# Picking expert tokens as rows by 512-column products, and expert comparisons moved beside a norm

## The reference

```python
g_w, g_idx = lax.top_k(softmax(xt @ w_group + b_group), 1)      # one of 4 groups
e_w, e_idx = lax.top_k(softmax(e_sel), 2)                       # 2 of its 4 experts
h = silu(einsum('nd,edf->nef', xt, w_gate)) * einsum('nd,edf->nef', xt, w_up)
h = h * combine[:, :, None]
y = einsum('nef,efd->nd', h, w_down)                            # D = 1024, F = 512
```

## Time and profile before

| | us |
|---|---|
| median of 3 runs | 1168.8 (1168.37 to 1170.16) |
| profiled execution | 1168.16 |
| its span | 1166.3 |
| PE busy | 1105.4 (95%) |
| DVE busy | 414.0 (36%) |
| ACT busy | 229.2 (20%) |

### The profile page before, as it was taken

One profiled execution on the slowest core, in us unless ns is written; L12 is line 12 of the kernel. 1 busy time (PEld: TensorE's weight loads), 2 busy tenths in 40 slices (PEclk: granted clock), 3 DMA queues, 4 the chain that ended last, 5 costly groups with the idle time before them and its releaser, 6 DMA issues.

```text
span 1166.3 us, 19793 instructions
## 1 busy us (share of the span) xinstructions
PE 1105.4 (95%) x8488; PEld 654.0 (56%) x8488; DVE 414.0 (36%) x1059; ACT 229.2 (20%) x531; POOL 128.3 (11%) x226
## 2 busy tenths in 40 slices
PE   4999999999899999999998899998999899999996
PEld 1666666666444576666654444444555656666562
DVE  2155656556712341000112655306863320000114
ACT  3111011011211321111111411115642411111110
POOL 0344434334100000000002000000000000000003
PEclk9999999999999999999999899999999999999999
DMA  9985444446842579999999920079770789999996
GB/s 346 291 292 149 136 146 146 146 146 217 338 187 89 180 270 423 411 428 427 424 427 348 368 102 1 18 258 371 263 281 18 253 353 418 429 426 424 425 418 227
DMA packets 102464, 321.27 MB, mean 275 GB/s; under 512 B 4048, under 2 KB 39168, under 8 KB 87008
## 3 DMA queue, kind: packets, MB, share of 16 engines
q1 hardware_dynamic: 93872, 298.05, 66.9%
q0 software_dynamic: 3248, 10.87, 2.8%
q10 hardware_dynamic: 5248, 10.98, 2.4%
HBM read 305.73 MB, written 14.16 MB: 274 GB/s over the span
## 4 chain that ended last, share of the span: by engine, by line
PE 80%; DMA 11%; DVE 4%; SPq 2%; issue 2%; ACT 1%; POOL 1%; POOLq 0%; ACTq 0%; DVEq 0%
PE bank L788 17%; PE bank L941 11%; PE bank L1181 11%; PE bank L811 7%; PE bank L678 7%; PE bank L777 6%; DMA ring<-in_moe_w_down 5%; PE bank L950 4%; PE bank L1067 4%; DMA ring<-in_w_ada 4%; PE bank L573 3%; PE bank L966 2%; PE bank L657 1%; DMA ring<-expert_rows,moe_row 1%; PE bank L664 1%
## 5 line engine op out<-in xcount | busy, mean ns | idle before, releaser
L788 PE MATMUL bank<-ring,xn 128*64 128x256 f32 x1472 | 163.5, 380 | 0.9 <-DMA ring<-in_moe_w_up 0.9
L788 PEld LDWEIGHTS bank<-ring,xn 128*64 128x64 f32 x1472 | 105.0, 137 | 61.4 <-issue 9.5
L941 PE MATMUL bank<-uT,ring 128*128 128x384 f32 x384 | 135.0, 496 | 0.0
L1181 PE MATMUL bank<-ring,uT 128*128 128x512 f32 x288 | 129.5, 603 | 4.3 <-DMA ring<-in_attn_w_qkv 2.7
L1869 DVE TENSOR_TENSOR moe_hh<-xn,bank 128x256 f32<-128x256 f32 x32 | 13.5, 421 | 291.7 <-ACT xn L1336 291.6
L811 PE MATMUL bank<-ring,xn 128*64 128x512 f32 x384 | 106.7, 596 | 0.9 <-ACT xn L1342 0.9
L941 PEld LDWEIGHTS bank<-uT,ring 128*128 128x128 f32 x384 | 69.2, 190 | 41.4 <-issue 1.1
L1181 PEld LDWEIGHTS bank<-ring,uT 128*128 128x128 f32 x288 | 54.1, 193 | 68.2 <-issue 64.1
L678 PE MATMUL bank<-ring,uT 128*128 128x512 f32 x192 | 84.1, 592 | 0.0
L777 PE MATMUL bank<-moe_g,moe_h 128*128 128x128 f32 x672 | 83.7, 282 | 0.5 <-DVE moe_g L1759 0.5
L777 PEld LDWEIGHTS bank<-moe_g,moe_h 128*128 128x128 f32 x672 | 79.9, 197 | 5.6 <-issue 5.6
(11 more groups left out here) (293 smaller groups left out, 1328.2 us busy)
## 6 DMA issues: line engine op xcount, KB each, us to landing
ring<-in_w_ada SPq DMA_DIRECT2D x24, 2048.0 KB, 12.1
ring<-in_moe_w_up SPq DMA_DIRECT2D x24, 2048.0 KB, 18.7
ring<-in_moe_w_gate SPq DMA_DIRECT2D x22, 2048.0 KB, 19.5
ring<-in_moe_w_down SPq DMA_DIRECT2D x21, 2048.0 KB, 19.9
ring<-in_hgrn_w_in SPq DMA_DIRECT2D x32, 512.0 KB, 6.9
moe_ring<-in_moe_w_gate SPq DMA_DIRECT2D x8, 2048.0 KB, 19.5
moe_ring<-in_moe_w_up SPq DMA_DIRECT2D x8, 2048.0 KB, 23.3
moe_ring<-in_moe_w_down SPq DMA_DIRECT2D x7, 2048.0 KB, 21.0
```

Of the source, the lines that this page charges most:

```text
L788: last = mm(bank[2 + e][64 * g:64 * g + 64, 256 * part:256 * part + 256], m["xe"][:, k, 64 * e:64 * e + 64], w[k][:, 256 * g:256 * g + 256 ...
L941: last = mm(to[:, 0:TOK], w[:, k, f, :], uT[:, k, :], start=(k == 0), stop=(k == KC - 1))
L1181: last = mm(bank[b % 2][:, :], uT[:, k, t * P:(t + 1) * P], cols(slot)[:, k, :], start=(k == 0), stop=(k == KC - 1))
```

## The change

It has two parts.

1. **Gather.** For pairs other than pair 1, `pick_rows(half, i)` now makes `moe_g` the stationary operand and `moe_h` the moving one: three products of 512 columns for each half give the picked tokens as rows (128 slots x 512 features) in bank 0 or 1. ACT (half 0) and DVE (half 1) copy them to `own[:, 1, :]` in the new step `picked`, and `gather(half, i)` then turns eight blocks of 128, as it did for pair 1 alone. `pick_rows(0, i+1)` stands behind the second gate/up product of pair i, `pick_rows(1, i+1)` behind the third; the turns stand where the gather stood. Pair 0 is picked and turned before the first body. POOL's fetch of pair 1 goes to the same place and waits until pair 0 has been turned. The counts of `gathered`, `xe_act` and `xe_dve` follow. (Further passes over the experts, which only a fuller expert needs, wait in `collect` for the slot of the last down weights.)
2. **Comparisons.** DVE's bias and comparisons are split by tiles: those of tiles 0 and 1 stand before the modulation of tile 2, their sums behind it, and only tile 2 is left for `experts`.

```diff
-GATHERS = 2 * PAIRS + FETCHED
+GATHERS = 4 * PAIRS - FETCHED
@@ PE, experts
+                def pick_rows(half, i):
+                    if half == 0:
+                        pe.wait_ge(s["onehot"], onehots_made(at_pass[0], i))
+                    for t in range(T):
+                        last = mm(bank[half][:, :], m["g"][:, t, :, :], m["h"][:, t, 512 * half:512 * half + 512],
+                                  start=(t == 0), stop=(t == T - 1))
+                    last.then_inc(s["gathered"], 1)
+
-                def gather(half, i):
+                def gather(half, i, it):
+                    if not fetched(i):
+                        pe.wait_ge((s["xe_act"], s["xe_dve"])[half], it * 2 + 1)
+                    elif half == 0:
+                        pe.wait_ge(s[f"rows{i}"], at_pass[0] * ROWS_IN[i] + 16)
                     for k in range(4):
-                        if 1 <= i <= FETCHED:
-                            here = slice((4 * half + k) * P, (4 * half + k + 1) * P)
-                            last = nc.tensor.transpose(bank[half][:, k * P:(k + 1) * P], m["own"][:, i, here], ident)
-                            continue
-                        for t in range(T):
-                            last = mm(bank[half][:, k * P:(k + 1) * P],
-                                      m["h"][:, t, (4 * half + k) * P:(4 * half + k + 1) * P],
-                                      m["g"][:, t, :, :], start=(t == 0), stop=(t == T - 1))
+                        here = slice((4 * half + k) * P, (4 * half + k + 1) * P)
+                        last = nc.tensor.transpose(bank[half][:, k * P:(k + 1) * P], m["own"][:, 1, here], ident)
                     last.then_inc(s["gathered"], 1)
@@ PE, body
                     gate_up(i, 0, 1, it)
+                    if picking:
+                        pick_rows(0, i + 1)
...
                     gate_up(i, 1, 0, it)
+                    if picking:
+                        pick_rows(1, i + 1)
                     if gating:
                         gate(n, m["diag"], 1, 2, 6)
                     gate_up(i, 1, 1, it)
                     if not last:
-                        gather(0, i + 1)
+                        gather(0, i + 1, it + 1)
@@ ACT, body
                         A(m["sg"][:, e, :], bank[2 + e][:, 0:256], ACT.Silu).then_inc(s["silu"], 1)
+                        if e == 0 and not last and not fetched(i + 1):
+                            picked(i + 1)
@@ DVE, second_norm and experts
                 second_norm(n, 2)
+                biased_logits(n, 0, 2)
+                compared(0, 2)
                 modulate(n, "xT2_done", "uT2_dve", 2, 1)
+                counted(0, 2)
...
-                need(dve, n, "logit_mm", 3)
...
+                biased_logits(n, 2, 3)
...
+                compared(2, 3)
+                counted(2, 3)
@@ POOL, fetch
+                        pool.wait_ge(s["gathered"], pair_gathered(p, 0, 1))
```

More of the change, by code:

```diff
@@ L843, in body @@
                 def body(i, it, first, last):
-                    pe.wait_ge(s["xe_act"], it + 1)
+                    pe.wait_ge(s["xe_act"], it * 2 + 2)
+                    picking = not last and not fetched(i + 1)
                     gating = i == GATE_PAIR and isinstance(it, int)
@@ L876, in body @@
                     if not last:
[L877 removed]
+                        gather(1, i + 1, it + 1)
                     pe.wait_ge(s["hT_ready"], it + 1)
@@ L884, in before @@
                     at_pass[0] = p
-                    gather(0, 0)
+                    pick_rows(0, 0)
+                    pick_rows(1, 0)
+                    gather(0, 0, p * PAIRS)
                     tokens_of(1)
-                    gather(1, 0)
+                    gather(1, 0, p * PAIRS)
                 def after(p):
@@ L1316, in rows, with picked @@
                     act.wait_ge(s["gathered"], pair_gathered(at_pass[0], i, 0))
-                    A(m["xe"][:, 0:4, :], bank[0][:, :], ACT.Copy).then_inc(s["xe_act"], 1)
+                    A(m["xe"][:, 0:4, :], bank[0][:, :], ACT.Copy).then_inc(s["xe_act"], 2 if fetched(i) else 1)
+                def picked(i):
+                    act.wait_ge(s["gathered"], rows_picked(at_pass[0], i, 0))
+                    A(m["own"][:, 1, 0:512], bank[0][:, :], ACT.Copy).then_inc(s["xe_act"], 1)
                 at_pass = [0]
@@ L1322, in before @@
                     at_pass[0] = p
+                    picked(0)
                     rows(0)
@@ L1663, in second_norm_end, with biased_logits, compared, counted @@
                 second_norm(n, 2)
+                biased_logits(n, 0, 2)
+                compared(0, 2)
                 modulate(n, "xT2_done", "uT2_dve", 2, 1)
+                counted(0, 2)
+            def biased_logits(n, start, stop):
+                need(dve, n, "logit_mm", stop)
+                own(v.tensor_tensor(MOE["lg"][:, start:stop, :],
+                                    bank[3][:, 20 * start:20 * stop].rearrange("p (t e) -> p t e", e=20),
+                                    brow[:, n, :].unsqueeze(1).broadcast_to([P, stop - start, 20]), ALU.add))
+            def compared(start, stop):
+                rows = slice(5 * start, 5 * stop)
+                shape = [P, 5 * (stop - start), 4, 4]
+                fives = MOE["lg"][:, start:stop, :].rearrange("p t (r j) -> p (t r) j", j=4)
+                each = fives.unsqueeze(3).broadcast_to(shape)
+                against = fives.unsqueeze(2).broadcast_to(shape)
+                own(v.tensor_tensor(MOE["equal"][:, rows, :, :], against, each, ALU.is_equal))
+                own(v.tensor_tensor(MOE["above"][:, rows, :, :], against, each, ALU.is_gt))
+            def counted(start, stop):
+                rows = slice(5 * start, 5 * stop)
+                shape = [P, 5 * (stop - start), 4, 4]
+                lower = const("lower").rearrange("p (j i) -> p j i", j=4).unsqueeze(1).broadcast_to(shape)
+                equal, above = MOE["equal"][:, rows, :, :], MOE["above"][:, rows, :, :]
+                own(v.tensor_tensor(equal, equal, lower, ALU.mult))
+                own(v.tensor_tensor(above, above, equal, ALU.add))
+                own(v.tensor_reduce(MOE["order"][:, rows, :], above, X_AXIS, ALU.add))
             def head_norm(n, tmp):
@@ L1704, in b4 @@
                     return a1.unsqueeze(2).broadcast_to([P, T, 4])
-                fives = m["lg"][:, :, :].rearrange("p t (r j) -> p (t r) j", j=4)
-                each = fives.unsqueeze(3).broadcast_to([P, 5 * T, 4, 4])
-                against = fives.unsqueeze(2).broadcast_to([P, 5 * T, 4, 4])
-                lower = const("lower").rearrange("p (j i) -> p j i", j=4).unsqueeze(1).broadcast_to([P, 5 * T, 4, 4])
-                v.tensor_tensor(m["equal"][:, :, :, :], against, each, ALU.is_equal)
-                own(v.tensor_tensor(m["above"][:, :, :, :], against, each, ALU.is_gt))
-                own(v.tensor_tensor(m["equal"][:, :, :, :], m["equal"][:, :, :, :], lower, ALU.mult))
-                own(v.tensor_tensor(m["above"][:, :, :, :], m["above"][:, :, :, :], m["equal"][:, :, :, :], ALU.add))
-                own(v.tensor_reduce(m["order"][:, :, :], m["above"][:, :, :, :], X_AXIS, ALU.add))
+                compared(2, 3)
+                counted(2, 3)
                 order = m["order"][:, :, :].rearrange("p (t r) j -> p t r j", r=5)
```

37 lines of the change are left out of this document (22 added, 15 removed).

## The result

The changed kernel took **1192.0 us** in the median of four runs (1191.05 to 1196.17), beside 1168.6 (1168.21 to 1170.16) for the kernel before: ratio **1.0205, 95% interval 1.0178 to 1.0231**, slower by some 23 us. The forecast of 1186.1 had the direction and most of the mechanism, and was 6 us short; the time lies at the upper edge of its range. The profiled execution took 1191.31 us, span 1189.5 against 1166.3. The kernel was measured again later beside the experiments, where the ratio was 1.0249 (1.0222 to 1.0276); what its trace shows there is told at the end of the experiments.

The account below looks back on a forecast made before the run. PE and DMA were taken to finish the expert stages together. Bodies 1 to 5 (+7.65), body 6 (+2.6), start and end give-backs made +8.8 and +9.1 us a layer: 1168.2 + 17.9 = 1186.1 us, range 1177 to 1192.

Parts of the forecast that it names:

- What bounds the kernel: Expert stages: PE and DMA arrive together; a slower PE is forgiven only 0.86 and 0.79 us at the weight waits.
- The picks, 12 x 429 = 5.15 us: Bodies 1 to 5: two picks between gate/up products, 12 records of 429 ns, cost 5.15 us a pair.
- Four times as wide saves 8%: Gather: products of 512 columns instead of 128 cost 0.84 ns a column against 0.91, saving 0.4 us a pair.
- The tail, 2.41 us: From last gate/up product to down products: turns and two uncovered short waits take 2.41 us instead of 6.03.
- that rival: Gather's turns follow each other at the pitch of their duration: 7 us a layer and more, 1200 us; chance 0.02.
- Body 6, +2.6 us with a new wait of 1.5: Pair 6: picks and tail add 1.06 us, and the third gate product waits 1.5 us for DVE.
- Start, -0.1: Stage start: comparisons save 0.75 us, pair 0's pick and turns add 0.65; net -0.1 us, within -1 and +1.
- What the end gives back, 1.41 and 1.12 us: Stage ends: lateness forgiven by weight waits and later waits, 0.86 + 0.55 us in layer 0, 0.79 + 0.33 in layer 1.
- A: Expert stages: loads bound them, so DMA hides PE's extra 1.5 us a pair; 1167 to 1171 us, chance 0.06.
- D: Shortened routing and cheaper picks win while DMA hides the turns; loads end earlier, 1165 to 1166 us, chance 0.03.
- B: Body 6's wait and part of each body's two short waits vanish; 1176 to 1180 us, chance 0.11.
- C: More loss: DMA idle from pair 1's slots freed later, or modulation pushed back; 1190 to 1195 us, chance 0.09.

Follow-up runs that it names:

- The column groups: Changed kernel with each pick cut into two halves of 64 columns, the form of the gate/up products around it; ratio 1.0126, +18.0 us at one clock.
- at the old place: Changed kernel with both picks behind the last gate/up product, where the gather was, and all eight turns behind the turns of hh; ratio 1.0029.
- moving the one copy: Changed kernel with DVE's copy of the picked rows in body 6 behind the two diagonals instead of before them; ratio 1.0178.
- the fillers: Kernel before plus unused PE products in bodies 1 to 5, 17.2 us or 8.6 us in all; ratios 1.0075 and 1.0043.

## Why the prediction was right and wrong

- **What bounds the kernel**: right. PE and the loads arrive together. A faster PE gives nothing that can be told from noise for 21 us less work; a slower one passes on all that goes beyond a slack of some 4 us.
- **The picks, 12 x 429 = 5.15 us: the step that failed.** The duration was read from a run of 32 equal records in the out projection, where nothing changes its form. Between gate/up products two picks cost 5.87 us. The term was mis-sized by 0.72 us; ten times over both layers that is 7.2 us, and the time was missed by 6. The right price stood in the trace before: products at 3.45 and 3.60 us, two gate records in 1.05. The rows of the gate products in body 6 were the nearest ones to a pick between gate/up products, nearer than the out projection. The column groups took the cost out and gave the forecast's 5.15 and, within a microsecond, its total. In body 6, where the picks share the excursion of the gate products, 5.15 was right.
- **Four times as wide saves 8%**: even less. In one piece at the old place the picks take 5.35 us, where the kernel before's gather took 2.88 and 2.68: 4%.
- **The tail, 2.41 us**: right (2.42), read from pair 0 of the kernel before. Turns follow each other at 0.11 to 0.13 us, not at their duration; that rival is out.
- **Body 6, +2.6 us with a new wait of 1.5**: right (+2.6, wait 1.4), and shown by moving the one copy.
- **Start, -0.1**: the comparisons gave 0.67 us of the 0.75 forecast at the marking of the experts and pushed nothing back, but only 0.06 of it was left at the first pick (the one-hots were to come 0.75 us earlier), since the clock's low spell had moved onto the routing. Pair 0 then kept 0.7 us in layer 0 and 0.55 in layer 1, because the pick ran at full clock, where the forecast had 1.4 us of slow records in it. In the later execution the spell fell on both. That the net stayed within a microsecond of the forecast is luck: the term is a matter of a spell that moves pair 0 by 2 to 3 us, and should have been a range of its own.
- **What the end gives back, 1.41 and 1.12 us**: too small in layer 0, where it was 2.4 us. In layer 1 it was 1.3, and the fillers give 3.8 to 4.3 for both together. The sentence that the wait for the next layer's weights forgives nothing was wrong: the second norm was 11.76 us late (657.40 against 645.64), the first product behind it 11.14.
- **Sum.** In layer 0 of the profile: start -0.7, bodies 1 to 5 5 x 2.33 = +11.7, body 6 +2.6, given back -2.4, together +11.2; forecast -0.1 + 7.65 + 2.6 - 1.41 = +8.8. The switches (+3.6 for the picks, +0.4 for other tenths in the bodies) outweigh the start and the slack that were better than thought.
- **Rivals.** A and D (the loads hide it) fall: no wait for weights is left. B (half) falls with the measured bodies. C named 1190 to 1195 us, but by other causes: the DMA's idle time or a modulation pushed back. The modulation moved by 0.08 us, and the filler, with which PE lets go of the slots later in the same way, costs no more than its work. C had the time, not the mechanism.

## What to carry to other kernels

Price a product by rows that have its neighbours, not only its size: where the rows before and behind it use the array in another form, look in the trace for the same neighbourhood, and compare one product's time in a row of its like with its time behind a stranger. Before moving work out of a gap, ask what it covered there; the new gather cost some 24 us with its picks between the products and 4 with them in the tail, where they hide two waits. Where two engines finish together, two doses of filler measure the slack better than the last wait of the trace does, since the slack has more than one link. And where a correction by the mean clock moves a result, compare the same stretches in the traces before believing it; when the same kernel reads differently a second time, compare its waits first.

## What the runs showed of the chip

- **A change of form costs about 0.35 us** on TensorE, in and out: between float32 products with a stationary tile of 64 columns in halves of the array and such of 128 over all of it. Entering it costs the strange records some 0.2 us (2.77 against 2.58), leaving it 0.15 (3.60 against 3.45). It shows in no row as idle time, only in the durations of the chain.
- **Run to run, time goes with the mean granted clock**, 0.85 us for each 0.001 (141 executions, scatter 1.1 us). The stage is at 0.98 to 1.00 in all profiles; what differs is the routing ahead of it, between 0.83 and 1.00 from 395 to 425 us, and the end. In one execution the 12 records of the first pick take 5.39 us and in another 7.02, part of them at 1.2 GHz instead of 2.4. Such a spell moved pair 0 by up to 3 us, more than the comparisons gain. What decides where it falls was not tested.
- **Behind its long gaps PE was also slow.** In the two kernels in which PE had been idle for 3.3 to 4.5 us before the down products of pair 7, the 16 records behind the gap took 5.46 to 5.82 us in all four places; behind the usual gap of 1.0 us they took 3.65 in the first profile. Such a gap cost about 2 us more than its length. A long gap is not the only way to slow records: both fillers had them (5.35) in layer 0 behind the usual gap.
- **A difference of 5 us between two measurements of one kernel** (+23.9 and +28.8 at one clock) is not explained by where the clock's spell falls in the routing alone. The second profile has the two late silus, which the first one lacks. Whether they account for the medians is not shown.
